# State-space stage: projection units in high/low form, the low parts made by GpSimd

## The reference, cut to what matters

```python
h = rmsnorm(x, mix_norm_w[i])
proj = h @ w_in[i]                       # 1024 -> 2816 columns and 12 time steps
y_s5  = s5_mixer(proj[..., :c_u], ...)    # 256 channels: complex scan over time
y_ssd = ssd_mixer(proj[..., c_u:c_z], proj[..., c_z:c_xbc], proj[..., c_xbc:], ...)
x = x + concatenate([y_s5, y_ssd], axis=-1) @ w_out[i]

def causal_dwconv(x, w, b):              # over the 14 x 128 xbc channels, 4 taps
    ...
```

## Time and profile before

| | |
|---|---|
| three runs, median | 2463.84 us (2461.8 to 2473.33) |
| the profiled execution | 2463.14 us, its span 2461.3 us |
| PE busy | 2364.9 us, 96% of the span |
| DVE / ACT / POOL busy | 1797.1 / 1157.5 / 148.3 us |
| the changed stage | from 1974.67 us to about 2132 us of the span |

### The profile page before, as it was taken

One profiled execution on the slowest core, in us unless ns is written; L12 is line 12 of the kernel. 1 busy time (PEld: TensorE's weight loads), 2 busy tenths in 40 slices (PEclk: granted clock), 3 DMA queues, 4 the chain that ended last, 5 costly groups with the idle time before them and its releaser, 6 DMA issues. The chain is left out here.

```text
span 2461.3 us, 36638 instructions
## 1 busy us (share of the span) xinstructions
PE 2364.9 (96%) x14280; PEld 2123.6 (86%) x14280; DVE 1797.1 (73%) x2913; ACT 1157.5 (47%) x1707; POOL 148.3 (6%) x141
## 2 busy tenths in 40 slices
PE   4979999999999999999999999999999999999998
PEld 4879898888888888889899888888888888898998
DVE  7979997677667676678999676566767576555665
ACT  4542255444545454564135444455545523544554
POOL 0000153000000000000045100000000000000000
PEclk9989999999999999999999999999999999999999
DMA  9365544787676666434544586665555523343553
GB/s 356 134 227 163 157 124 149 267 298 240 233 242 231 239 231 223 148 111 139 177 135 125 188 299 220 204 216 187 189 188 191 191 78 108 124 148 126 189 186 107
DMA packets 133554, 460.63 MB, mean 187 GB/s; under 512 B 15152, under 2 KB 16432, under 8 KB 132912
## 3 DMA queue, kind: packets, MB, share of 16 engines
q1 hardware_dynamic: 133424, 458.90, 55.1%
HBM read 445.73 MB, written 13.11 MB: 186 GB/s over the span
## 5 line engine op out<-in xcount | busy, mean ns | idle before, releaser
L1654 DVE TENSOR_TENSOR ring_lo<-ring,ring_hi 128x1024 fp32r<-128x1024 f32 x421 | 506.9, 1222 | 88.6 <-ACT ring_hi L1557 88.6
L1557 ACT ACTIVATE ring_hi<-ring 128x1024 fp32r<-128x1024 f32 x421 | 435.0, 1054 | 134.0 <-PE banks L346 119.9
L319 PE MATMUL banks<-normed_lo,ring_hi 128*128 128x512 f32 x1344 | 477.9, 398 | 0.0
L344 PE MATMUL banks<-ring_hi,work_lo 128*128 128x512 f32 x1024 | 400.5, 391 | 8.0 <-DVE work_lo L1681 4.3
L345 PE MATMUL banks<-ring_lo,work_lo 128*128 128x512 f32 x1024 | 399.9, 391 | 0.0
L346 PE MATMUL banks<-ring_hi,work_lo 128*128 128x512 f32 x1024 | 399.1, 390 | 0.0
L320 PE MATMUL banks<-normed_lo,ring_lo 128*128 128x256 f32 x1344 | 377.2, 281 | 0.0
L319 PEld LDWEIGHTS banks<-normed_lo,ring_hi 128*128 128x128 f32 x1344 | 252.5, 188 | 61.8
L361 DVE TENSOR_TENSOR ring_lo<-ring,ring_hi 128x1024 fp32r<-128x1024 f32 x185 | 225.0, 1222 | 78.1 <-ACT ring_hi L356 77.5
L320 PEld LDWEIGHTS banks<-normed_lo,ring_lo 128*128 128x128 f32 x1344 | 253.8, 189 | 3.3
L1677 DVE TENSOR_TENSOR work<-banks,work 128x512 f32<-128x512 f32 x84 | 58.1, 692 | 249.2 <-ACT work L1563 249.2
(11 more groups left out here) (387 smaller groups left out, 4357.4 us busy)
## 6 DMA issues: line engine op xcount, KB each, us to landing
ring<-wstream SPq DMA_DIRECT2D x716, 512.0 KB, 3.3
arena<-wstream SPq DMA_DIRECT2D x96, 512.0 KB, 5.7
spill<-one_hots SPq DMA_DIRECT2D x44, 256.0 KB, 4.2
rstd<-spill SPq DMA_DIRECT2D x16, 256.0 KB, 4.1
pool_and_keys<-spill SPq DMA_DIRECT2D x14, 256.0 KB, 4.1
routes<-spill SPq DMA_DIRECT2D x14, 256.0 KB, 4.8
residual<-xT SPq DMA_DIRECT2D x1, 1024.0 KB, 7.8
arena<-mixconst SPq DMA_DIRECT2D x2, 512.0 KB, 4.2
```

Source lines behind the costliest of these rows:

```text
L319: pe.matmul(dst, w_hi[:, o], HR[:, k, :], start=(k == 0), stop=(k == KD - 1), skip_group_check=True)
L344: pe.matmul(dst, hi[:, t], w_hi[:, o], start=first, stop=False)
L1557: sc.activation(RING_HI[:, u % HIGHS, :], RING[:, u % SLOTS, :], ACT.Copy)\
L1654: dve.tensor_tensor(RING_LO[:, u % SLOTS, :], RING[:, u % SLOTS, :], RING_HI[:, u % HIGHS, :].bitcast(F32), ALU.subtract).then_inc(S("spli ...
```

## The change

The 22 input units take the split form too.

- Units 0 to 2: high parts by ACT and low parts by DVE at the end of the expert stage before, as other stages have it; PE multiplies them in `unit_group`, ahead of `time_steps`.
- Units 3 to 21: ACT makes a unit's high part behind the drain of the unit four places earlier, POOL its low part (L1887 of the changed kernel) when the high part is there; `project(i)` waits for it (`in_low`) and is a `unit_product`.
- DVE makes the input's low parts (`norm_flow`), ACT its high parts (`high_flow`). `time_steps` reads the unsplit `H32`.
- PE's order: projections 3 to 6 stay where they were; 7 to 21 each stand one place earlier, in the place of the one before, and the last place, ahead of `ssd_output(0)`, is empty.
- `XP` moves to the arena, over `M`, which is written after the convolutions. The high parts of the output units then follow the drains 18 to 21 like any others, without a wait for the convolutions.

```diff
-                    if layer + 1 < DEPTH:
-                        for i in range(PRE):
-                            high(N_EXP + i, 0)
+                    for i in range(PRE):
+                        high(N_EXP + i, 0)
...
-                    if layer + 1 < DEPTH:
-                        for i in range(PRE):
-                            low(N_EXP + i, 0)
+                    for i in range(PRE):
+                        low(N_EXP + i, 0)
...
-        XP = HOT.rearrange("p a b -> p (a b)")[:, 0:14 * (T + 3)].rearrange("p (c t) -> p c t", c=14)
+        XP = AR[:, m_at:m_at + 14 * (T + 3)].rearrange("p (c t) -> p c t", c=14)
+        N_REST = N_IN2 - PRE
...
                 for t in (XP, XD):
                     pool.memset(t, 0.0).then_inc(S("cleared"), 1)
+                for i in range(N_REST):
+                    u = I_IN + PRE + i
+                    pool.wait_ge(S("high"), i + 1)
+                    pool.tensor_tensor(RING_LO[:, u % SLOTS, :], RING[:, u % SLOTS, :],
+                                       RING_HI[:, u % HIGHS, :].bitcast(F32), ALU.subtract).then_inc(S("in_low"), 1)
...
-                    if i >= 3:
-                        pe.wait_ge(S("drained"), i - 2)
-                    arrived(pe, I_IN + i)
-                    for k in range(KD):
-                        if i == 0:
-                            pe.wait_ge(S("h_scaled"), k + 1)
-                        mm = pe.matmul(PS[:, 2 + i % 3, 0:T], RING[:, (I_IN + i) % SLOTS, k * P:(k + 1) * P], H[:, k, :],
-                                       start=(k == 0), stop=(k == KD - 1))
-                    mm.then_inc(units_used, 1)
+                    pe.wait_ge(S("drained"), i - 2)
+                    pe.wait_ge(S("in_low"), i - PRE + 1)
+                    unit_product(pe, PS[:, 2 + i % 3, 0:T], I_IN + i, H_HI, H_LO).then_inc(units_used, 1)
...
-                project(0)
-                project(1)
+                unit_group(pe, range(I_IN, I_IN + PRE), [PS[:, 2 + i, 0:T] for i in range(PRE)], (True,) * PRE)
                 time_steps()
                 s5_input(0)
                 s5_input(1)
-                project(2)
                 project(3)
...
-                project(15)
+                project(16)
                 inner(0)
-                project(16)
+                project(17)
                 s5_output(6)
                 inner(1)
...
                 act = Steps(sc, S)
+                high_flow(act, H32, None)
+                split_high(act, I_IN + PRE, False)
                 act.wait("cleared", 2)
...
                         act.mark(sc.activation(ZU[:, i - FIRST_Z + 2, :], src, ACT.Silu), "drained")
+                    split_high(act, I_IN + i + HIGHS, False)
...
-                for k in range(KD):
-                    flow_scaled(v, H, V2[:, W_MIX:W_MIX + 8], k)
+                norm_flow(v, H32, V2[:, W_MIX:W_MIX + 8], None)
```

More of the change, by code:

```diff
@@ L1858, in program @@
         ER1 = a(12, P)
+        m_at = a.at
         M = a(12, 384)
@@ L1925, in time_steps @@
                         for k in range(KD):
-                            mm = pe.matmul(PS[:, 5, tt * 12:tt * 12 + 12], H[:, k, tt * P:(tt + 1) * P], WDT[:, k, :],
+                            mm = pe.matmul(PS[:, 5, tt * 12:tt * 12 + 12], H32[:, k, tt * P:(tt + 1) * P], WDT[:, k, :],
                                            start=(k == 0), stop=(k == KD - 1))
@@ L2032, in _ @@
                 project(6)
+                project(7)
                 s5_output(1)
@@ L2035, in _ @@
                 rows(2)
-                project(7)
+                project(8)
                 rows(3)
-                project(8)
+                project(9)
                 s5_output(2)
@@ L2041, in _ @@
                 rows(4)
-                project(9)
+                project(10)
                 rows(5)
-                project(10)
+                project(11)
                 s5_output(3)
                 s5_input(5)
-                project(11)
                 project(12)
+                project(13)
                 s5_output(4)
                 s5_input(6)
-                project(13)
                 project(14)
+                project(15)
                 s5_output(5)
                 s5_input(7)
-                project(15)
+                project(16)
                 inner(0)
-                project(16)
+                project(17)
                 s5_output(6)
                 inner(1)
-                project(17)
+                project(18)
                 inner(2)
                 s5_output(7)
-                project(18)
+                project(19)
                 inner(3)
-                project(19)
+                project(20)
                 turn_x(0)
                 turn_x(1)
-                project(20)
+                project(21)
                 turn_x(2)
                 turn_x(3)
-                project(21)
                 for i in range(4):
@@ L2177, in _ @@
                 drain(18)
-                act.wait("convolved", 14)
-                split_high(act, I_OUT, True)
-                split_high(act, I_OUT + 1, True)
                 drain(19)
-                split_high(act, I_OUT + 2, True)
                 drain(20)
-                split_high(act, I_OUT + 3, True)
                 drain(21)
@@ L2351, in _ @@
                 decayed(3)
-                split_low(v, I_OUT, 0)
+                split_low(v, I_OUT, N_REST)
                 weight_x(0)
                 weight_x(1)
-                split_low(v, I_OUT + 1, 1)
+                split_low(v, I_OUT + 1, N_REST + 1)
                 weight_x(2)
                 weight_x(3)
-                split_low(v, I_OUT + 2, 2)
+                split_low(v, I_OUT + 2, N_REST + 2)
                 gate_y(0)
-                split_low(v, I_OUT + 3, 3)
+                split_low(v, I_OUT + 3, N_REST + 3)
                 for i in range(1, 4):
@@ L2390, in _ @@
                     if i + HIGHS < 8 + PRE:
-                        split_low(v, I_OUT + i + HIGHS, i + HIGHS)
+                        split_low(v, I_OUT + i + HIGHS, N_REST + i + HIGHS)
                 token_inverse(v)
```

## The result

The median of six runs is 2489.18 us for the changed kernel and 2463.08 us for the kernel before. One slow run of the changed kernel, 3399.57 us at a mean granted clock of 0.65, is left out of all that follows: its other five have a median of 2488.81 us. The ratio is 1.0100, 95% interval 1.0089 to 1.0111. The profiled execution took 2488.81 us too, its span 2487.0 us, 25.7 us more than before.

A forecast was written before the change was run, and what follows sets the result against it. PE's instruction stream was taken to set the pace, DVE close behind. First decayed step +21.0 us, less 6.4 behind it, plus 2.5 for the clock: +17.1 on 2463.84, so 2481 us, own range 2472 to 2488, widened to 2456 to 2488.

The forecast's parts named there:

- from it to the time steps: Stage start: interleaved scaled and low parts and three units ahead delay the time steps, moving the first turn 2.3 us later.
- blocked steps: DVE's chain: 14 meetings with POOL's subtractions, each costing 1.8 us, 25.2 us in all.
- The deciding term: POOL's nineteen subtractions and DVE's steps with two SBUF inputs exclude each other: 25.2 us in DVE's chain.
- the bound of 2.56: Upper bound in us for one POOL subtraction, allowing for a full second read; 2.08 was taken.
- the contending 47.6 us: DVE's busy time in two-SBUF-input steps (convolutions, sum, scans, second products), 70% of its 67.2 us.
- The tail: First decayed step to first SSD output: PE sets the pace again and saves 6.4 us; lower clock costs 2.5.
- two signs: For a time above 2488 us: POOL's step longer than 2.56 us, or PE losing its clock more than once.
- What was costed at nothing: High and low copies ending the expert stage, hidden in idle ACT and DVE, and XP's move: no cost; uncovered copies, 3.5 us.
- The ring: Unit transfers: no limit, as a unit takes fewer us but stays far from what one transfer takes.
- DVE yields nothing: Rival: POOL and DVE's scans and convolutions get past each other, so not slower, 2455 us; 13%.
- POOL takes only the gaps: Rival: exclusion holds, but POOL's steps fit under DVE's 19.6 us of other work; +3.0, 2467 us; 12%.
- PE's whole saving arrives: Rival: DVE's waits shrink and the start is not later, so all 13.0 us are saved, 2451 us; 3%.

The follow-up runs named there:

- e6_pool_added: Kernel before plus nineteen POOL subtractions of 1024 elements whose output nothing uses, all but the first behind a drain: 2487.05 us against 2463.89.
- e2_dve_low: Changed kernel with the nineteen low parts made by DVE instead of POOL, nothing left out: 2474.29 us, ratio 1.0033 to the kernel before.
- e7_tail_and_group: Kernel before with input units 17 to 21 split and units 0 to 2 as a split group, 14 units plain: 2462.62 us, ratio 0.9992.
- e1_no_low: Changed kernel without POOL's low parts of units 3 to 21; the third product rereads the high part: 2459.10 us against 2465.53 for the kernel before.
- e3_pool_copy: Changed kernel with POOL copying the high part, one input, instead of subtracting for units 3 to 21: 2468.98 us, ratio 1.0014 to the kernel before.
- e4_quarters: Changed kernel with each POOL low part made in four instructions of 256 columns: 2479.39 us, ratio 1.0052 to the kernel before.
- e5_tail: Kernel before with only input units 17 to 21 split, POOL's low parts starting after the last convolution: 2460.51 us against 2463.89.

## Why the prediction was right in kind and short in size

The sum again, by its own terms, with what the changed kernel's trace has for each:

| term | forecast | measured |
|---|---|---|
| DVE's first step of the stage | 0 | +1.45 |
| from it to the time steps: 11.7 instead of 9.4 | +2.3 | +2.3 (11.72) |
| time steps to first turn | 0 | +1.2 (5.88 instead of 4.71) |
| chain: 67.2 of DVE's own plus blocked steps | 67.2 + 25.2 | 67.2 + 29.9 + 0.3 |
| first decayed step | +21.0 | +28.6 |
| from there on, clock included | -6.4 + 2.5 = -3.9 | -4.0 |
| after x_mixed | 0 | +1.1 |

**The deciding term held in mechanism.** Total exclusion, by whole instructions, also for scans and three-operand steps, which no row of before showed: e6_pool_added and the maxima of 2.8 us show it. 16 POOL steps fell into the chain, as counted. By the Trainium skill's page SBUF — State Buffer, section "Who interferes with whom", the port pair that DVE and POOL share is an exclusive lock: whoever issues first has it for the whole instruction, and the other blocks fully. The traces agree (0.68 us becomes 2.86; 0.18 becomes 2.28).

**It was mis-sized by 4.7 us, in two factors:** the term of 14 x 1.8 = 25.2 us measured 15 x 1.99 = 29.9. POOL's step is 2.40 us, not 2.08. I took the lower value because the row of before had 512 elements in 1.04 us, with a small, repeated second operand. The step is 15% longer than twice that row, inside the bound of 2.56; no run changes the second operand alone, so how much of the 15% is its full read stays open. The prediction's estimate from the Trainium skill's page GPSIMD Engine Reference, section "Elementwise — side-by-side cycle accounting", 2.25 us, was nearer than mine and still 0.15 short. And 15 steps were blocked, not 14, at 1.99 us each instead of 1.8. The fifteenth count matters less than where three of them fell: on 24-element steps right after the first turn, where POOL had three low parts in a row. I had left small steps out of the contending 47.6 us, as they are 0.18 us each. What a blocked step costs is the other engine's length, so a short step is as costly as a long one.

**Two terms were missing at the start**, 2.6 us together, both of the clock. The stage's first step is 1.45 us late, since the clock fell earlier in the norm's sums ahead of it. Timeline of PE, the norm's sums, the kernel before and the changed one:

```profile
1968.54 3.76 PE L427 MATMUL banks<-consts_sb,normed 128*128 128x1 f32 x32 [0.41 <-DVE residual L1843]
```

```profile
1968.70 5.06 PE L427 MATMUL banks<-consts_sb,normed 128*128 128x1 f32 x32 [0.41 <-DVE residual L1841]
```

In the windows 1968 to 1971 and 1971 to 1974 the granted clock is 1.00 and 0.68 before, 0.97 and 0.50 here. It does not follow the change: from PE's first sum to DVE's first step the norm takes 6.1 us in the kernel before, and also in e2_dve_low and e7_tail_and_group, which have the changed end of the expert stage; it takes 7.4 here, and also in e6_pool_added, whose program up to there is that of before (e1_no_low 7.5, e3_pool_copy 7.2, e4_quarters 6.3, e5_tail 6.1). Why it differs between executions stays open. Behind the group of three the clock falls as well, from the end of the time steps on, while the first S5 inputs run; the prediction took this stretch from a row at full clock. Windows of 3 us, granted clock third from last, first the changed kernel, then the kernel before at the same place in its program (its S5 input starts at 1987.56):

```profile
1990.00:1993.00 3.00, 3.00 (x18) 2.73 (x18) 1.44 (x2) 1.23 (x1) 3.00 (x2) 0.72 0.81 309
1993.00:1996.00 3.00, 3.00 (x15) 2.62 (x15) 2.83 (x7) 0.22 (x1) 0.44 (x1) 0.71 0.06 22
```

```profile
1987.00:1990.00 3.00, 3.00 (x18) 2.74 (x18) 1.77 (x5) 0.22 (x1) 0.00 (x0) 1.00 0.00 1
```

The eight S5 matmuls took 3.65 us instead of 1.97. The same fall is in e1, e2, e3 and e7 (3.3 to 3.6 us for these matmuls), not in e4 (1.97), and in none of the three kernels without the group. With one exception among six it goes with the group; that the group brings it about is not shown.

**The tail was right**, the saving of 6.4 and what the clock takes of it. PE stood still for 11.5 us ahead of `inner(1)` (12 forecast), and the clock was at its lower level (0.50) from about 2080 until about 2097. The split unit behind that wait took 4.2 us instead of 2.86. For a time above 2488 us the prediction had named two signs. A POOL step longer than 2.56 us is not what happened, except where DVE held one (2.79 at most). That PE loses its clock more than once is: in the windows above the granted clock is 0.79, 0.95, 0.75 and 0.82 where the kernel before has 1.00 from 1990 to 2110. In DVE's chain this cost nothing, as the chain is made up of DVE's own steps and the holds but for 0.3 us.

**The last 1.1 us** lies behind x_mixed, in stages that the change does not touch. From x_mixed to the end of the span three profiles have 347.1 to 347.6 us (before, e5_tail, e7_tail_and_group) and the other six 348.1 to 348.9. The clock parts them in the same way: in the 12 us around the start of the attention stage the granted clock is 0.86 in the three and 0.72 in the six (2132 to 2144 us before, 2156.65 to 2168.65 here). So this too goes with the clock. What makes it fall for longer there stays open; it is not the loss in the chain, as e1_no_low is among the six.

**What was costed at nothing** was nothing: behind the copies at the end of the expert stage, PE goes from its last transposes to the norm's first sum in 2.35 us (1966.35 to 1968.70), as before (1966.19 to 1968.54), and e1_no_low keeps ACT's high copies and the moved `XP` without a step of DVE being longer. The ring was no limit either: no wait of the stage is put down to a transfer. But a transfer is not as far from a unit's time as the prediction has it: a unit takes 3.3 us from issue to landing (median of both pages) and 2.86 us on PE.

**The rivals.** *DVE yields nothing* would have looked like e1_no_low, and the changed kernel does not. *POOL takes only the gaps* fell with POOL's own times: it was POOL that held. *PE's whole saving arrives* needed a shorter chain on DVE; even without a contest it ended at 70.2 us.

## What to carry to other kernels

Before moving work to GpSimd beside a busy VectorE, list VectorE's steps in that stretch by where their inputs lie: each with two SBUF inputs, however small, may be held for the whole length of a GpSimd instruction that reads SBUF, and the loss is about the number of meetings times that length. It can be cheaper to let the busy engine do the work itself (1.22 us against 2.0 us lost), and GpSimd's help held nothing up where VectorE read PSUM (five steps, in e5_tail). If such work must lie there, cut it into short instructions (8.5 us less in the chain here), and see whether the engine that got the relief was the one that bounds the stage.

## What the runs showed of the hardware that I had not expected

- A POOL subtraction with two full inputs takes 2.34 to 2.42 us for 1024 columns undisturbed, a copy 1.04 (1.10 on average, with those that DVE held). Pieces of 256 columns take 0.71 us at the least and 905 ns on average, waits for DVE included.
- A one-input step of DVE can be held too. `TENSOR_SCALAR` on 24 elements, 0.18 us before, beside POOL's pair of steps:

```profile
1988.78 4.65 POOL L1887 TENSOR_TENSOR ring_lo<-ring,ring_hi 128x1024 fp32r<-128x1024 f32 x2 [3.36 <-ACT ring_hi L356]
...
1991.74 1.73 DVE L2290 TENSOR_SCALAR arena<-arena 128x24 f32<-128x24 f32 x1
```

  It ended with POOL's pair, at about 1993.4. It cost next to nothing, since the first turn had to wait for PE's slow S5 input anyway (5.88 us behind the time steps; 5.74 in e1_no_low, where nothing is held). The Trainium skill's page SBUF — State Buffer, section "Who interferes with whom", names `tensor_scalar` among the operations that can enter a 2-port mode and so contend with a single input, under conditions on the operands. In e4_quarters the same step (its L2293) took 0.54 us beside POOL's quarters; no run here tests the conditions.
- The granted clock can fall while PE's row shows it busy without a gap: 3.00 of 3 us at 0.72 in the window above.
